# Low halves of the weight slabs by an accumulating transfer onto -whi, in place of GpSimd's subtraction

## What is computed

```python
for l in range(DEPTH):
    h = rmsnorm(x, pre_g[l])
    proj = jnp.einsum('bsd,de->bse', h, w_in[l])
    u_a, v_a, g_a, q, k, v, g_b = jnp.split(proj, idx, axis=-1)
    y_a = gmlp_group(u_a, v_a, ln_a_g[l], ln_a_b[l], spatial_w[l], spatial_b[l]) * jax.nn.silu(g_a)
    y_b = gqa_axial_attention(q, k, v, q_norm_g[l], k_norm_g[l], tables) * jax.nn.silu(g_b)
    y = jnp.concatenate([y_a, y_b], axis=-1)
    out = jnp.einsum('bse,ed->bsd', y, w_out[l])
    x = x + rmsnorm(out, post_g[l])
```

```python
xn = rms_norm(h, norm_gain[l])
proj = xn @ w_in[l]
...
y_sb = (o_sb * jax.nn.silu(sb_z)) @ w_branch_sb[l]
y_sw = (o_sw * jax.nn.silu(sw_z)) @ w_branch_swa[l]
merged = jax.nn.sigmoid(g_sb) * y_sb + jax.nn.sigmoid(g_sw) * y_sw
h = h + merged @ w_out[l]
```

## Time and profile before

| | |
|---|---|
| median of 3 runs | 1251.65 us (1250.45 to 1254.59) |
| span of the profiled execution | 1249.3 us |
| TensorE busy | 1087.2 us, 87% |
| VectorE busy | 725.3 us, 58% |
| ScalarE busy | 470.0 us, 38% |
| GpSimd busy | 342.2 us, 27% |
| mean granted clock of TensorE | 0.946 |

### The profile page before, as it was taken

How to read it: one execution, slowest core, us unless ns; L and a number is a source line. 1 busy time by engine, 2 the same in 40 slices (tenths; PEclk the granted TensorE clock), 3 DMA queues, 4 the chain that set the end, 5 groups by cost and what they waited for, 6 DMA issues and landing times.

```text
span 1249.3 us, 16958 instructions
## 1 busy us (share of the span) xinstructions
PE 1087.2 (87%) x6437; PEld 942.7 (75%) x6437; DVE 725.3 (58%) x1264; ACT 470.0 (38%) x830; POOL 342.2 (27%) x119
## 2 busy tenths in 40 slices
PE   4995799888679679987859999999998988999995
PEld 4994677678679567767858778788986776888895
DVE  5299777833819877783482366675745787222115
ACT  3324144413222434450424476662335455222211
POOL 3244110042324411013322120212343242332330
PEclk9999699989789879998979899999999999999998
DMA  6420201122052120112222120121331010322321
GB/s 198 151 72 31 85 1 51 35 68 69 24 165 69 34 84 18 34 34 85 78 84 68 34 68 1 35 67 35 102 101 50 2 35 1 102 94 90 101 69 68
DMA packets 81829, 81.05 MB, mean 65 GB/s; under 512 B 7488, under 2 KB 79296, under 8 KB 81744
## 3 DMA queue, kind: packets, MB, share of 16 engines
q1 hardware_dynamic: 80272, 78.09, 19.9%
q10 hardware_dynamic: 1472, 1.84, 0.4%
HBM read 77.82 MB, written 2.10 MB: 64 GB/s over the span
## 4 chain that ended last, share of the span: by engine, by line
PE 56%; DVE 22%; issue 12%; ACT 5%; POOL 4%; DMA 1%; POOLq 0%; DVEq 0%; SPq 0%; ACTq 0%
PE ps L1420 14%; PE ps L1421 13%; PE ps L1422 13%; POOL wlo L426 2%; PE ps L1453 2%; PE ps L1455 2%; PE ps L1454 2%; PE ps L1550 2%; PE ps L1681 2%; ACT pw L841 2%; DVE pwt L1177 1%; DVE t L970 1%; DVE vn L1002 1%; DVE t L962 1%; DVE small L1355 1%
## 5 line engine op out<-in xcount | busy, mean ns | idle before, releaser
L426 POOL TENSOR_TENSOR wlo<-raw,whi 128x2048 fp32r<-128x2048 f32 (+1 forms) x34 | 150.2, 4422 | 398.3 <-ACT whi L490 398.3
L452 POOL TENSOR_TENSOR wlo<-raw,whi 128x2048 fp32r<-128x2048 f32 (+1 forms) x31 | 135.9, 4386 | 363.7 <-ACT whi L674 363.7
L1420 PE MATMUL ps<-whi,hhi 128*128 128x256 f32 x544 | 159.6, 293 | 34.4 <-DVE hlo L914 22.9
L1421 PE MATMUL ps<-wlo,hhi 128*128 128x256 f32 x544 | 157.9, 290 | 0.0
L1422 PE MATMUL ps<-whi,hlo 128*128 128x256 f32 x544 | 157.7, 290 | 0.0
L1420 PEld LDWEIGHTS ps<-whi,hhi 128*128 128x128 f32 x544 | 108.9, 200 | 37.0 <-issue 14.3
L1420 PE MATMUL ps<-hhi,whi 128*128 128x512 f32 x288 | 114.9, 399 | 2.5 <-ACT tg L856 1.7
L1421 PE MATMUL ps<-hlo,whi 128*128 128x512 f32 x288 | 113.7, 395 | 0.0
L1422 PE MATMUL ps<-hhi,wlo 128*128 128x512 f32 x288 | 113.7, 395 | 0.0
L1421 PEld LDWEIGHTS ps<-wlo,hhi 128*128 128x128 f32 x544 | 108.9, 200 | 0.0
L1422 PEld LDWEIGHTS ps<-whi,hlo 128*128 128x128 f32 x544 | 108.4, 199 | 0.0
(11 more groups left out here) (270 smaller groups left out, 2713.3 us busy)
## 6 DMA issues: line engine op xcount, KB each, us to landing
raw<-in_w_in SPq DMA_DIRECT2D x45, 1024.0 KB, 5.3
raw<-in_w_out SPq DMA_DIRECT2D x12, 1024.0 KB, 5.0
raw<-in_w_branch_swa SPq DMA_DIRECT2D x4, 1024.0 KB, 5.0
raw<-in_w_in SPq DMA_DIRECT2D x4, 512.0 KB, 5.1
raw<-in_w_branch_sb SPq DMA_DIRECT2D x4, 512.0 KB, 3.5
out<-x SPq DMA_DIRECT2D x4, 512.0 KB, 2.6
x<-in_x SPq DMA_DIRECT2D x2, 512.0 KB, 5.9
x<-in_x ACTq DMA_DIRECT2D x2, 512.0 KB, 7.5
```

The costliest lines, as they stand in the source:

```text
L426: pool.tensor_tensor(wlo[s][:, :, 0:w], raw[s][:, :, 0:w], whi[s][:, :, 0:w].bitcast(F32), ALU.subtract).then_inc(slab_split, 1)
L452: pool.tensor_tensor(wlo[s][:, 0:n, :], raw[s][:, 0:n, :], whi[s][:, 0:n, :].bitcast(F32), ALU.subtract).then_inc(slab_split, 1)
L1420: pe.matmul(out_ap, lhsT=lhi(k), rhs=rhi(k), start=first and k == 0, stop=False, skip_group_check=True)
L1421: pe.matmul(out_ap, lhsT=lhi(k), rhs=rlo(k), start=False, stop=False, skip_group_check=True)
```

## The change

The low half is made in two steps. ScalarE, behind whi, writes a second copy of raw, with scale -1, to wlo: it is -whi, rounded as whi is. Then GpSimd issues a transfer from raw to wlo that adds to what it finds there, waits until it has landed (`lo_added`), and raises `slab_split`. A slab of 128 columns goes in four transfers. `whi_done` now stands behind the second copy. GpSimd issues and waits for slabs 20, 24, 28 and 32 of the second block too.

```diff
@@ module, semaphores @@
-DVE_SLABS = [20, 24, 28, 32]
...
+        lo_asked, lo_added = sem("lo_asked"), sem("lo_added")
...
@@ GpSimd, split_lo @@
                 pool.wait_ge(whi_done, l * SLABS + i + 1)
                 w = IN_SLABS[i % SLABS][1] if i % SLABS < len(IN_SLABS) else 256
                 s = i % RING
-                pool.tensor_tensor(wlo[s][:, :, 0:w], raw[s][:, :, 0:w], whi[s][:, :, 0:w].bitcast(F32),
-                                   ALU.subtract).then_inc(slab_split, 1)
+
+                pool.sem_inc(lo_asked, 1)
+                step = KT if w == 256 else 2
+                for k in [slice(k, k + step) for k in range(0, KT, step)]:
+                    pool.dma_start(wlo[s][:, k, 0:w].bitcast(F32), raw[s][:, k, 0:w], accum_op=ALU.add)\
+                        .then_inc(lo_added, 8 * step)
+                pool.wait_ge(lo_added, l * (64 * SLABS) + 64 * (i + 1))
+                pool.sem_inc(slab_split, 1)
...
@@ GpSimd, split2_lo @@
                 pool.wait_ge(whi_done, DEPTH * SLABS + j + 1)
-                pool.tensor_tensor(wlo[s][:, 0:n, :], raw[s][:, 0:n, :], whi[s][:, 0:n, :].bitcast(F32),
-                                   ALU.subtract).then_inc(slab_split, 1)
+                pool.dma_start(wlo[s][:, 0:n, :].bitcast(F32), raw[s][:, 0:n, :], accum_op=ALU.add).then_inc(lo_added, 64)
+                pool.wait_ge(lo_added, 64 * (DEPTH * SLABS + j + 1))
+                pool.sem_inc(slab_split, 1)
...
-            for j in range(21, len(SLABS2)):
-                if j in DVE_SLABS:
-                    continue
-                if j - 1 in DVE_SLABS:
-
-                    pool.wait_ge(slab_split, DEPTH * SLABS + RING + j)
+            for j in range(20, len(SLABS2)):
                 split2_lo(j)
...
@@ ScalarE, split_hi @@
-                act.activation(whi[s][:, :, 0:w], raw[s][:, :, 0:w], ACT.Copy).then_inc(whi_done, 1)
+                act.activation(whi[s][:, :, 0:w], raw[s][:, :, 0:w], ACT.Copy)
+                act.activation(wlo[s][:, :, 0:w], raw[s][:, :, 0:w], ACT.Copy, scale=-1.0).then_inc(whi_done, 1)
...
@@ ScalarE, split2 @@
-                act.activation(whi[s][:, 0:n, :], raw[s][:, 0:n, :], ACT.Copy).then_inc(whi_done, 1)
+                act.activation(whi[s][:, 0:n, :], raw[s][:, 0:n, :], ACT.Copy)
+                act.activation(wlo[s][:, 0:n, :], raw[s][:, 0:n, :], ACT.Copy, scale=-1.0).then_inc(whi_done, 1)
...
@@ VectorE, gates @@
             for g in range(4):
-                j = DVE_SLABS[g]
-                dve.wait_ge(whi_done, DEPTH * SLABS + j + 1)
-                dve.wait_ge(slab_split, DEPTH * SLABS + RING + j)
-                low(wlo[j % RING][:], raw[j % RING][:], whi[j % RING][:]).then_inc(slab_split, 1)
                 for c in (2 * g, 2 * g + 1):
```

## The result

The changed kernel takes **1348.13 us** (median of 4 runs, 1342.72 to 1351.06) against 1251.05 us for the kernel before on the same chip (1250.21 to 1254.59): a ratio of 1.0776, 95% interval 1.0739 to 1.0813, 97 us slower. The forecast was 21 us slower. The sign was right and 1348 lies inside the range (1225 to 1365), but the size was off by more than a factor of four. That it lies inside is luck: the range was made that wide for a slower transfer, X up to 11.5 us, and that is not what happened.

What follows compares the result with a forecast made beforehand. TensorE, busy 87%, was taken to bound the kernel, GpSimd's subtraction costing more through VectorE than by its length. Layers -4.1 and -13.2, block 2's start -2.5, the rest +41.2: +21.4 on 1251.65, so 1273 us, range 1225 to 1365.

Steps and rivals of the forecast that it cites:

- X: Time of a 1 MB transfer from GpSimd's issue to its semaphore, taken as 8.0 us; the sign turns at 6.9.
- +3.8 at the output slabs: Slabs 12 to 15 of each layer: 1.6 us gained by slabs 12 and 13, slab 15's cycle 5.4 longer.
- -16.5 in the first layer: Rope and vn, each layer: VectorE freed from GpSimd's subtraction, so TensorE's waits shrink by 17.5 us, less about 1.0.
- the wait before z: TensorE's 10.96 us wait ahead of the z products, ended by VectorE; was to be gone or under 2 us.
- Slab 0: 12.9 (end of whi) + 1.9 + 8.0 = 22.8; ... Together +8.2: First layer's start: slab 1 ready 2.8 us later, slab 2 another 5.4 later, together 8.2 us lost.
- -2.5: Block 2's start, like the second layer's: 6.0 us gained through VectorE, 3.5 lost again.
- A half slab is then 2 + 3 = 5.0: Transfer time of a half slab: 2 us fixed and 3 us of data, 5.0 us.
- the second layer repeats it: VectorE ends TensorE's 10.96 us wait before z in the second layer too, so -16.5 us counts there again.
- block 2 to the gates, +6.9: Block 2 to 1055: stick-breaking part +3.5 us, chosen rather than summed, dense slabs +3.1, slab 19's half transfer +0.3.
- Faster: Rival, chance 0.28: the transfer is little slower than a load, X under 6.7; some 1230 us at X = 5.8.
- Slower by far: Rival, chance 0.27: GpSimd's preparing of a transfer stands behind VectorE's operations, X 10, 1325 us.
- No release: Rival, chance 0.05: issuing or waiting holds the port as the subtraction does, VectorE's savings are gone, 1318 us.

Runs made afterwards that it cites:

- e3_starts: The changed kernel with slabs 0 and 1 of each of the three starts made by GpSimd's subtraction again; 1328.10 us, ratio 1.0626 to the kernel before.
- e1_half: The changed kernel with slabs 10 and 11 of each layer contiguous, each in one transfer instead of four; 1330.36 us, ratio 1.064 to the kernel before.
- e9_loads: The changed kernel with SyncE's six small loads moved behind its loads of slabs 2 and 3; 1346.38 us, ratio 1.0794 to the kernel before.
- e5_plain: The changed kernel with plain transfers of zeros in place of the adding ones, low halves left out; 1267.02 us, ratio 1.0128 to the kernel before.
- e10_more: The kernel before with transfers for slabs 3 to 13 of each layer, half ones contiguous, and six slabs of block 2; 1227.18 us, ratio 0.9831.
- e7_three: The changed kernel with contiguous half slabs, the gates' four slabs on VectorE and each start's slabs 0 and 1 by GpSimd's subtraction; 1275.06 us, ratio 1.0198.

## Why the prediction was wrong

*X.* Right: 7.4 to 7.6 us undisturbed against 8.0 in the sums, inside "6.7 to 9" (6.9 from issue to semaphore, at the edge of "wrong if X is outside 6.9 to 9"). The path's terms that rest on it alone came out: 5.2 against 5.4 at slab 2 (e3_starts), +3.7 and +3.2 against +3.8 at the output slabs (e1_half), 6.0 us of waiting against 7.1 at slab 24, +6.7 against +6.0 at the last slabs. The new waits of "about 6 us" before slabs 2, 15, 24, 28, 32 and 36 are 5.4 to 6.0 us. Right too: VectorE's 5.22 us back to 0.82, -15.6 against -16.5 in the first layer, though the wait before z kept 2.31 us where it was to be "gone or under 2".

*First failed step: "Slab 0: 12.9 (end of whi) + 1.9 + 8.0 = 22.8; ... Together +8.2".* It let X hold at any place of the program. At slab 0 the transfer took 21.3 us, and slab 1's 10.3. Measured +27.6; with the small loads out of its way slab 0 began at 22.6 and the total was +15.4, of which 4.9 us are the same loads beside slab 2's transfer (e9_loads). The trace before spoke of it: its list of issues has 16.4 to 18.0 us to landing for the biases, ws and the gains of q and k, so that they were in flight at 15 to 30 us. But I asked only how a slab's load would fare ("so they stay hidden") and not how the new transfer would fare behind other loads. At block 2's start, -2.5 became +10.2: slab 1's transfer is issued at 667.4, 0.7 us behind the load of slab 2, and takes 12.0 us. Subtracting the first two slabs there leaves +4.5 (e3_starts).

*Second: "A half slab is then 2 + 3 = 5.0".* That scaled the bytes and forgot that the diff's loop makes four transfers, whose fixed part GpSimd pays one after another: 13.3 us. It is worth 10.7 and 10.4 us in the two layers (e1_half against the changed kernel), of which block 2 takes some 3 away again.

*Third: a term that the sum lacked.* Each wait of TensorE was priced by its length. The trace has 28.7 us of added busy time for the same matmuls, 2.6 us behind the wait of 6 us at slab 24. The Trainium skill ("TensorE: Matmul & The Clock Gate", Part 1) says that the lower clock is the default and activity releases it; this case's rows agree, 0.80 behind a wait of 6 us against 1.00 without. In e5_plain 17.5 of the 78.5 us by which its span is shorter are such busy time (1098.4 us). No term of the sum had this.

*Fourth: "the second layer repeats it".* It did not: before the change, TensorE's wait for vn in the second layer was 6.01 us, where the earlier trace rows has 10.96, so that only 11.7 came. It stood in the trace of the kernel before (VectorE's two vn products take 5.12 us here and 10.07 in the earlier trace rows):

```profile
433.94 5.12 DVE L1002 TENSOR_TENSOR vn<-t,vn 128x512 fp32r<-128x512 f32 x2 [0.70 <-ACT vn L569]
...
439.20 0.55 PE L1420 MATMUL ps<-wst,vn 128*128 128x256 f32 x1 [6.01 <-DVE vn L1002]
```

*Fifth: block 2 to the gates, +6.9.* Measured +14.0. The +3.5 "chosen rather than summed" for the stick-breaking part was near (+2.8 measured). The dense slabs cost 6.2 us instead of 3.1, and 4.8 lie within slab 17, for which the sum had 0.3, where GpSimd's wait for slab 18 holds pw; the rows and e10_more point to it, no run isolates it. I had looked at slab 19 (+0.3) and not at 18.

*The rivals.* "Faster" needed X under 6.7; the plain transfer reached that and the kernel was still 1.3% slower, so the claim that X alone decides the sign was wrong as well: slab 0's transfer and the pieces had prices of their own. "Slower by far" named the size nearly (1325) but by a mechanism that the trace does not have: the issuing instruction takes 0.85 to 0.88 us at all 35 transfers of block 2, whether VectorE is busy or not, and slab 6's transfer (118.8 to 125.4) lands in 6.6 us with VectorE working back to back from 118.6 on. "No release" is out. The Trainium skill ("Collectives: The Full Stack", the section on the bandwidth ceiling) says that two source reads halve the rate. Here it fell from 338 to 202 GB/s, a factor of 0.6, and 202 GB/s are 12.6 for each of the 16 engines: the rule's direction holds, the 15.5 that the prediction took from it was too good for this transfer.

**Still open.** What the first transfer waits for while the DMA engines are mostly idle; two places show that it is slow while the small loads are under way, and no run shows by what means. Why TensorE's clock was lower in one stretch of e9_loads. And 25 us that are left in e7_three, which no run takes apart.

## What to carry to other kernels

A transfer between buffers in place of an engine's operation pays where the operation holds another engine and the result is needed late: slabs 3 to 13 here, 2.3% faster. Where TensorE waits for the result, 1.9 us of a second copy and 7.4 to 7.6 of the transfer, instead of 4.6 to 4.7, count in full, and then the slower clock behind the wait counts too. Price each transfer at its own place in the program: how many instructions the loop really issues, what else is in flight at that moment, and which work stands in the issuing engine's queue behind its wait. A layer that runs the same code isn't the same timeline: read the second one's waits as well.

## What the runs showed of the hardware

- An adding transfer of 1 MB from SBUF to SBUF, issued by GpSimd: first packet 1.4 us after issue, landing at 6.6; 202 GB/s. The plain one of the same size: 1.1, 4.2 us, 338 GB/s.
- Pieces of 128 KB in rows of 512 bytes: one every 3.4 to 3.6 us with the add, with the DMA engines busy for a share of 0.41 of that stretch (below). The same half slab in one piece lands in 4.2 us, and the four pieces without the add in 5.9.

```profile
225.00:236.50 11.50, 11.50 (x59) 9.31 (x57) 9.36 (x20) 4.25 (x11) 3.59 (x3) 1.00 0.41 46
```

- A transfer of GpSimd's had its first packet 14.2 us after its issue while SyncE's and ScalarE's loads in short rows were under way, with the DMA engines 30% busy. Beside SyncE's alone, in e9_loads, it was 4.7 us and 11.5 to landing. The load of a whole slab beside it is milder: slab 3's transfer, issued 0.6 us behind such a load, takes 9.9 us instead of 6.6.
